# Softmax factors applied to the probabilities on VectorE, and two gate products moved ahead of the attention loop

## The reference, cut to what matters

```python
s = jnp.where(ok, einsum('bqhd,bkhd->bhqk', q, k) * scale + bias, NEG_INF)
p = jax.nn.softmax(s, axis=-1)                 # exp(s - max) / sum
o = jnp.einsum('bhqk,bkhd->bqhd', p, v)
# NSA heads: three such attentions (compressed, selected, window), each with its gate
out = g[..., 0:1] * o_c + g[..., 1:2] * o_s + g[..., 2:3] * o_w     # g = sigmoid(gate_logits)
# merge of the three branches, 1024 columns each
gates = sigmoid(merge_logits + b_merge)        # merge_logits = h @ w_in[:, 3072 columns]
mixed = gates[0] * (out_a @ w_o_nsa) + gates[1] * (out_b @ w_o_mla) + gates[2] * (out_c @ w_o_fox)
x = x + mixed @ w_out
x = x + hier_moe(rmsnorm(x), ...)              # 32 experts, all weights read: 96 MB a layer
```

## Time and profile before

| what | us |
|---|---|
| runs | 1117.98, 1119.61, 1119.73 (median 1119.61) |
| the profiled execution, its time | 1120.61 |
| its span | 1118.6 |
| PE busy | 981.9 (88%) |
| DVE busy | 256.9 (23%) |
| ACT busy | 213.6 (19%) |
| attention loop with its head, layer 0 | 132.53 to 268.38 |
| the same in layer 1 | 681.66 to 817.79 |

### The profile page before, as it was taken

The page is one execution under the profiler, slowest core; times in us unless marked ns, Lnnn a source line. Parts: engine busy times, 40 slices in busy tenths (PEclk is TensorE's granted clock), DMA queues, the critical chain, the costliest instruction groups (busy, mean ns, idle before and its releaser), DMA issues. The chain is left out here.

```text
span 1118.6 us, 14392 instructions
## 1 busy us (share of the span) xinstructions
PE 981.9 (88%) x5943; PEld 705.9 (63%) x5943; DVE 256.9 (23%) x918; ACT 213.6 (19%) x561; POOL 24.6 (2%) x68
## 2 busy tenths in 40 slices
PE   7999899999999966677799998999999998666666
PEld 6888688788887333333289877888888854223222
DVE  2210422323423111110121123223234231001102
ACT  1211345442002100000011113444400210000001
POOL 0000000000000000000010000000000000000000
PEclk9999999999999988888899999999999999888888
DMA  9977232535955999999996441425388469999992
GB/s 290 274 164 245 76 113 82 183 113 207 347 195 201 423 421 421 421 421 421 345 270 204 139 123 38 151 86 178 114 308 331 151 265 421 422 421 421 421 421 121
DMA packets 122759, 289.94 MB, mean 259 GB/s; under 512 B 13390, under 2 KB 84164, under 8 KB 100164
## 3 DMA queue, kind: packets, MB, share of 16 engines
q1 hardware_dynamic: 119472, 286.25, 68.9%
q10 hardware_dynamic: 3220, 2.74, 1.5%
HBM read 286.35 MB, written 2.62 MB: 258 GB/s over the span
## 5 line engine op out<-in xcount | busy, mean ns | idle before, releaser
L781 PE MATMUL bank<-tail,ring 128*128 128x256 f32 x1280 | 291.7, 384 | 0.0
L781 PEld LDWEIGHTS bank<-tail,ring 128*128 128x128 f32 x1280 | 241.5, 192 | 39.3 <-issue 7.5
L1559 PE MATMUL bank<-ring,tail 128*32 128x512 f32 x896 | 123.2, 713 | 102.1 <-DMA ring<-in_moe_w_up 102.1
L1559 PEld LDWEIGHTS bank<-ring,tail 128*32 128x32 f32 x896 | 35.3, 129 | 189.7 <-issue 189.7
L1032 PE MATMUL bank<-tail,ring 128*128 128x256 f32 x384 | 83.4, 380 | 0.0
L1801 DVE SCALAR_TENSOR_TENSOR tail<-tail,bank 128x256 f32<-128x256 f32 x16 | 6.7, 422 | 319.8 <-ACT tail L1680 319.8
L1032 PEld LDWEIGHTS bank<-tail,ring 128*128 128x128 f32 x384 | 72.8, 190 | 10.2 <-issue 0.3
L1122 ACT ACTIVATE ring<-ring,small 128x128 f32<-128x128 f32 (+1 forms) x128 | 56.6, 443 | 76.5 <-DVE small L1363 76.5
L1532 PEld LDWEIGHTS bank<-tail 128*128 128x128 f32 x512 | 61.6, 200 | 12.9 <-issue 12.2
L1532 PE MATMUL bank<-tail 128*128 128x128 f32 x512 | 65.0, 287 | 0.8 <-DVE tail L1739 0.5
L1631 PE MATMUL bank<-ring,tail 128*32 128x512 f32 x512 | 58.2, 595 | 0.6 <-DVE tail L1812 0.6
(11 more groups left out here) (256 smaller groups left out, 783.3 us busy)
## 6 DMA issues: line engine op xcount, KB each, us to landing
ring<-in_moe_w_gate SPq DMA_DIRECT2D x64, 1024.0 KB, 26.2
ring<-in_moe_w_up SPq DMA_DIRECT2D x64, 1024.0 KB, 26.3
ring<-in_moe_w_down SPq DMA_DIRECT2D x64, 1024.0 KB, 23.4
ring<-in_w_in SPq DMA_DIRECT2D x48, 1024.0 KB, 7.8
ring<-in_w_out SPq DMA_DIRECT2D x8, 1024.0 KB, 10.0
ring<-in_w_o_mla SPq DMA_DIRECT2D x4, 1024.0 KB, 5.1
ring<-in_w_o_fox SPq DMA_DIRECT2D x4, 1024.0 KB, 5.1
ring<-in_w_o_nsa SPq DMA_DIRECT2D x4, 1024.0 KB, 5.1
```

The lines of the kernel that those rows point to most:

```text
L781: last = pe.matmul(dst, weight(k), hT[:, k, :], start=(k == 0), stop=(k == KD - 1))
L1559: last = pe.matmul(bank[4][CAP * e:CAP * e + CAP, :].rearrange("p (a f) -> p a f", a=2), XT[:, g % 2, k, CAP * e:CAP * e + CAP], ring[:, l ...
```

## The change

On DVE `row_factors` becomes `normed`: the reciprocal of the four sums; in SLC and WIN a product of these four with the gates; then two products in place that multiply the probabilities of the first query tile (2x128 columns) and of the second (2x256 columns) by the row's factor. It now stands ahead of `shifted(u+1)` in DVE's loop. `unit_out(u)` becomes a copy out of the bank (FOX, MLA) or one addition, and comes one iteration later. On PE `turn` loses the two transposes of the factors, and waits for `normed` alone. ACT copies 384 columns of each bank and not 512. The gate products are numbered on from `AHEAD = 2`: product 0 stands ahead of the transposes of the compressed probabilities, product 1 between `scores(0)` and `scores(1)`, and the loop has a second product in every third unit (0, 3, ... 15), where it was every second. `scores(0)` no longer waits for ACT's copies of the compressed output.

```diff
+    AHEAD = 2
     def gates_at(u):
-        q = u + (u + 1) // 2
-        return q, (q + 1 if u % 2 == 0 else None)
+        q = AHEAD + u + (u + 2) // 3
+        return q, (q + 1 if u % 3 == 0 else None)
...
                 last.then_inc(s_fb, 1)
+            pe.wait_ge(s_mqte, 4)
+            gate_logits(0)
             pe.wait_ge(s_pc, 1)
...
             def turn(u):
-                pe.wait_ge(s_exp, u + 1)
+                pe.wait_ge(s_rs, u + 1)
                 if u:
                     pe.wait_ge(s_pta, u)
                 for half in range(2):
                     for i in range(3):
-                        pe.transpose(bank[4 + half][:, i * P:(i + 1) * P],
-                                     prob[u % 3][:, half, i * P:(i + 1) * P], ident)
-                pe.wait_ge(s_rs, u + 1)
-                for t in range(NT):
-                    last = pe.transpose(bank[4 + t][:, 3 * P:4 * P],
-                                        rwide[:, t].rearrange("p s d -> p (s d)"), ident)
+                        last = pe.transpose(bank[4 + half][:, i * P:(i + 1) * P],
+                                            prob[u % 3][:, half, i * P:(i + 1) * P], ident)
                 last.then_inc(s_pt, 1)
...
-            pe.wait_ge(s_mqte, 4)
+            scores(0)
+            gate_logits(1)
             pe.wait_ge(s_oce, 2)
-            scores(0)
             for u in range(UNITS):
...
             def turned(u):
                 act.wait_ge(s_pt, u + 1)
                 if u >= 2:
-                    act.wait_ge(s_oe, u - 1)
+                    act.wait_ge(s_pv, u - 1)
                 for half in range(2):
-                    last = act.activation(probT[:, u % 2, half, :], bank[4 + half][:, :], ACT.Copy)
+                    last = act.activation(probT[:, u % 2, half, :], bank[4 + half][:, 0:3 * P], ACT.Copy)
...
             probabilities(0)
+            for q in range(AHEAD):
+                gate_tanh(q)
...
-            def row_factors(u):
+            def normed(u):
                 br, c = divmod(u, 4)
                 dve.wait_ge(s_exp, u + 1)
                 s(dve.reciprocal(rs[:, 4 * u:4 * u + 4], sm[:, 4 * u:4 * u + 4]))
                 s.sync()
-                if u:
-                    dve.wait_ge(s_pt, u)
-                r = bc(factors(rs, u), [P, NT, 2, DH])
-                if br < SLC:
-                    dve.tensor_copy(rwide, r).then_inc(s_rs, 1)
-                else:
-                    dve.tensor_tensor(rwide, r, bc(gates[:, :, c, :, br - SLC + 1], [P, NT, 2, DH]), ALU.mult)\
-                       .then_inc(s_rs, 1)
+                if br >= SLC:
+                    r = factors(rs, u)
+                    s(dve.tensor_tensor(r, r, gates[:, :, c, :, br - SLC + 1], ALU.mult))
+                    s.sync()
+                for t in range(NT):
+                    lo, hi = seg(t)
+                    pr = prob[u % 3][:, :, lo:hi]
+                    last = dve.tensor_tensor(pr, pr, bc(factors(rs, u)[:, t, :], [P, 2, hi - lo]), ALU.mult)
+                last.then_inc(s_rs, 1)
             def unit_out(u):
                 br, c = divmod(u, 4)
                 dve.wait_ge(s_pv, u + 1)
-                o = two(bank[6 + u % 2])[:, 0, :].rearrange("p (t c) -> p t c", t=NT)
-                spread = probT[:, u % 2, :, 3 * P:4 * P]
+                o = bank[6 + u % 2][:, 0:T]
                 acc = oT[:, (2, 1, 0, 0)[br], c, :]
                 if br < SLC:
-                    dve.tensor_tensor(acc.rearrange("p (t c) -> p t c", t=NT), o, spread, ALU.mult).then_inc(s_oe, 1)
+                    dve.tensor_copy(acc, o).then_inc(s_oe, 1)
                 else:
-                    s(dve.tensor_tensor(otmp.rearrange("p (t c) -> p t c", t=NT), o, spread, ALU.mult))
-                    s.sync()
-                    dve.tensor_tensor(acc, acc, otmp, ALU.add).then_inc(s_oe, 1)
-                    dve.wait_ge(s_oe, u + 1)
+                    if br == WIN:
+                        dve.wait_ge(s_oe, u - 3)
+                    dve.tensor_tensor(acc, acc, o, ALU.add).then_inc(s_oe, 1)
...
-            for u in range(UNITS + 1):
+            for u in range(UNITS + 2):
+                if u < UNITS:
+                    normed(u)
                 if u + 1 < UNITS:
                     shifted(u + 1)
-                if u < UNITS:
-                    row_factors(u)
-                if u >= 1:
-                    unit_out(u - 1)
+                if u >= 2:
+                    unit_out(u - 2)
```

More of the change, by code:

```diff
@@ L185, in program @@
     mtmp = kept(7168, 2, T)
-    otmp = kept(7168, T)
-    rwide = kept(7424, NT, 2, DH)
     wrt = kept(7680, KD, LW)
@@ L213, in program @@
     qrt = region(12288, 4, NT * H * HALF)
-    probT = region(13056, 2, 2, 512)
+    probT = region(13056, 2, 2, 384)
     mp = region(14592, NT, M_W)
@@ L912, in attention_tensor, with gate_logits @@
                 last.then_inc(s_mqt, 1)
+            def gate_logits(q):
+                if q % 2 == 0:
+                    att_wait(pe, L_MG + q // 2)
+                if q >= 2:
+                    pe.wait_ge(s_gt, q - 1)
+                wm = slot_cols(L_MG + q // 2, 256)
+                columns(bank[2 + q % 2][:, 0:T], lambda k: wm[:, k, (q % 2) * P:(q % 2 + 1) * P]).then_inc(s_mgl, 1)
             pe.wait_ge(s_mve, 2)
```

## The result

| | before | after |
|---|---|---|
| median of the runs, us | 1118.80 (1117.60 to 1119.73, 4 runs) | 1102.05 (1101.76 to 1102.26, 4 runs) |
| profiled execution, its span | 1118.6 | 1100.2 |
| ratio of the times | | 0.9847, 95% interval 0.9835 to 0.9859 |

The change makes the kernel 16.8 us faster; 1103.8 was forecast, in a range from 1100.8 to 1109. One of the ten executions of the kernel before in a later experiment took 1448.17 us at a mean granted clock of 0.65, and its ratio leaves it out. Put side by side by landmarks, the two profiled executions show where the time went. The merge starts at the first merge product, the experts at the first product of the experts' gate and up weights.

What follows compares the result with a forecast made beforehand. PE was taken to bound attention and DMA the expert stages. Savings of 7.99 us in layer 0 and 8.27 in layer 1, together 16.3, gave 1104.3 from the profiled execution and 1103.3 from the median; forecast 1103.8, range 1100.8 to 1109.

Steps and rivals of the forecast that it cites:

- 1, transposes in the loop: In each layer's loop, 15 units lose the two factor transposes on PE, 0.22 us a unit: 3.30 us a layer saved.
- 2 and 3, two products less and the end: Two gate products leave the loop, 6.90 us; the last values product's wait for ACT's copies shrinks, 0.44 us; a layer.
- 4, new head: From the forget-gate products to `scores(2)`: 19.38 us with two more gate products in it, against 16.73 and 17.01 before.
- 4, clock in the head: The head's sum takes the clock as full, since 0.71 us is the only gap left of 3.85.
- 5, VectorE's work: `normed` on DVE takes 1.5 us a unit, 1.7 with gates, covered by some 4 us free: cost zero.
- experts: Experts wait for DMA; an earlier PE starts their weight stream earlier by the same amount, and its length stays.
- the rival on DMA: The expert stage swallows part: at most 1.4 us of new backlog a layer, 2.8 in all, 1106.6 us; chance 0.04.
- The slower rival: The chain exponentials, `normed`, turn becomes the loop once `normed` takes over 5.6 us; 1134 us at 6.6; chance 0.02.

Runs made afterwards that it cites:

- the gate products alone: The kernel before with the gate products placed as in the change and the factors still spread and transposed as before: 1109.42 us, ratio 0.9920.
- The experiment with four more products: The changed kernel with four more VectorE products of 512 columns in each unit, written to unused space: 1113.65 us, ratio 0.9954 to the kernel before.
- two more products: The changed kernel with two more VectorE products of 512 columns in each unit, written to unused space: 1101.77 us, ratio 0.9845 to the kernel before.

## Why the prediction was right

Its sum held term by term against the profile that it was worked out from. In microseconds a layer:

| step | forecast | measured |
|---|---|---|
| 1, transposes in the loop | 3.30 | 3.28 (changed kernel against the gate products alone) |
| 2 and 3, two products less and the end | 7.34 | 7.51 (119.12 - 111.61) |
| 4, new head | 19.38 | 19.47 |
| 4, clock in the head | full | full, in both profiles |
| 5, VectorE's work | 0, hidden | 0, no turn waits |
| experts | pass the gain on | passed on |

The 0.09 in the head is made of small items of both signs: gate products 0 and 2 take 3.35 and 3.34 and not 3.45, the transposes behind product 0 with the wait 1.07 and not 0.96, L946 with its gap 1.92 and not 1.76. VectorE's work is 1.2 us in a unit without gates, not 1.5. In the rival on DMA, "0.98" should read 1.01 (170.91 less 0.17 and less 169.73), which changes nothing.

The time came out 1.75 us under the 1103.8 forecast. Of that 1.3 is the starting point: the forecast subtracted its 16.3 from 1120.1, the middle of the profiled execution and the median of three runs, where the median of the four runs is 1118.80. Two things were not seen rightly.

The clock was priced as if the head of before always lost it. That gave the right sum for the profile at hand, but it is a chance: of four heads of that kernel in two profiles three fell. Without any fall a layer of before takes 139.98 us from the forget-gate products to the merge (layer 0 of its second profile), and the changed kernel 133.57. So 6.41 us a layer, 12.8 in all, are work and gaps. The other 4 of the 16.8 measured are a difference; falls of the clock that no longer come are what the profiles offer for it. Filling two gaps of the head without any other change won 3.0. A part of the falls came as a surprise: in the profile of before the clock also fell in the router part behind the merge, 0.6 us in each layer. It did so in five of the ten profiles of the other kernels too, in one layer or both; no instruction there was changed, and why the changed kernel's two profiles have no such fall stays open. So that the medians differ by 16.8, close to the 16.3 of the sum, is partly luck: the sum counted a fall in every head, which does not come in every one, and none behind the merge, where some do.

The falls may also be why the kernel before scatters over 3 us (1117.5 to 1120.8) and the changed one over less than 2 (1101.4 to 1103.2), but they do not explain every scatter: the kernel with the gate products alone has the new head and spread from 1107.54 to 1113.11 over six executions.

The slower rival had its point of decision at the wrong place. Step 5 gave the factors "some 4 us" of cover by following one unit from its scores to its turn, and let the rival decide at 5.6 us. The experiment with four more products, 4.06 us for `normed` in an MLA unit (187.82 to 191.88), was already 11.6 us slower. The turn's slack is one limit; the other is the ring of shift, exponentials and factors, since DVE starts no shift before it has finished the factors of the unit before. With the factors as they are the ring takes 4.5 to 4.7 us (7.39 or 7.57, less the 2.90 of the four products) and PE's unit 7.22, so some 2.6 us are free. By this estimate the point is between 3.7 and 3.9 us (4.06 less 7.57 or 7.39, plus 7.22); the runs show only that 2.7 us (two more products) are hidden and 4.06 are not. The forecast did not lean on this, because the real work was 1.2 us.

## What to carry to other kernels

When work moves between engines, compute two margins: how late one item may come, and the ring, the shortest period in which the engines can hand over item after item, against the mean period of the busiest engine. When TensorE is the bound, independent products belong into its waits, at the head of a loop first: they win the wait, and they keep the clock from falling, which here was worth some 3 of the 16.8 us. And a price read off one profile for a fall of the clock is one draw: take a second profile of the same kernel before it enters a sum.

## What the runs showed of the hardware

- Dummy matmuls in two gaps (under 1.2 and under 2 us long) made the kernel 0.3% faster, with nothing else changed.
- The same code had its clock at 1.00 and at 0.90 in the same stretch: 15.09 against 17.04 us in the two layers of one execution, and 15.09 against 16.73 us in layer 0 of two executions.
- A float32 product in place on VectorE with a factor repeated along the columns takes 0.685 us for 512 columns and 0.425 for 256. An addition of 256 columns without a repeated operand took 0.425 too, so at that size the repetition costs nothing that shows.
- Where the tile's shape on TensorE changes between 64 rows, 64 columns and full, a gap of 0.17 to 0.33 us stands in most places; between 96 rows and full none is listed ahead of the full tile (166.28 in the earlier trace rows). No run changed the shape alone, so that the shape is the cause is not shown. In the changed kernel's loop of layer 0 these 9.4 us are all the waits that the profile lists for PE's weight loads (total us, times, longest):

```profile
PEld bank L781 <- issue: 3.5, 11, 0.3
PEld bank L996 <- issue: 3.3, 15, 0.3
PEld bank L971 <- issue: 2.6, 14, 0.3
```
